# Placing the bias loads later in SyncE's order of loads, dilated stage of a four-block network, one core

## What is computed

```python
proj = (h @ w_in).reshape(B, S, N_DIL_GROUPS, 3, DIL_HEADS, DIL_HEAD_DIM)   # 3 groups, q/k/v, 16 heads, 64
for gi, (window, dilation) in enumerate(((128, 1), (512, 4), (2048, 16))):
    q = rms_norm(proj[:, :, gi, 0], g_q[gi]); k = rms_norm(proj[:, :, gi, 1], g_k[gi]); v = proj[:, :, gi, 2]
    # inside dilated_group: scores plus a bias gathered from a table by distance, softmax over the window
    s = einsum(q, k) * DIL_HEAD_DIM ** -0.5 + bias
    lse = logsumexp(s); p = exp(s - lse); o = einsum(p, v)
o = sum over the groups of softmax(lse over the groups) * o
y = o.reshape(B, S, 1024) @ w_o
```

## Time and profile before

| | us |
|---|---|
| median of 3 runs | 3462.44 |
| lowest and highest | 3458.5, 3465.23 |
| the profiled execution | 3470.18 |
| its span on the core | 3468.1 |
| PE busy in the span | 3271.7 (94%) |
| dilated stage, 826 to 1431 us of the span: PE busy | 574.05 of 605.00 |

### The profile page before, as it was taken

The page is one execution under the profiler, slowest core; times in us unless marked ns, Lnnn a source line. Parts: engine busy times, 40 slices in busy tenths (PEclk is TensorE's granted clock), DMA queues, the critical chain, the costliest instruction groups (busy, mean ns, idle before and its releaser), DMA issues.

```text
span 3468.1 us, 60606 instructions
## 1 busy us (share of the span) xinstructions
PE 3271.7 (94%) x24316; PEld 2519.5 (73%) x24316; DVE 1967.9 (57%) x2468; ACT 1259.1 (36%) x2175; POOL 1276.5 (37%) x729
## 2 busy tenths in 40 slices
PE   6899999999999989999999998888899999999998
PEld 4455678887766767778888887666578787578877
DVE  8457566555464555655554675555466455854444
ACT  3345331224554555531223434333322224242222
POOL 0134434444655544334443322000245443034443
PEclk9999999999999999999999999888999999999999
DMA  6424145443434333244443221000155343023332
GB/s 239 123 89 128 49 135 192 155 168 111 124 110 118 110 88 98 73 152 169 157 169 91 67 62 48 10 13 19 32 188 193 128 157 111 13 81 96 96 91 84
DMA packets 281139, 376.33 MB, mean 109 GB/s; under 512 B 59830, under 2 KB 208987, under 8 KB 269659
## 3 DMA queue, kind: packets, MB, share of 16 engines
q1 hardware_dynamic: 276568, 359.31, 32.8%
q10 hardware_dynamic: 4354, 13.98, 1.0%
HBM read 357.49 MB, written 15.73 MB: 108 GB/s over the span
## 4 chain that ended last, share of the span: by engine, by line
PE 73%; issue 8%; DVE 7%; POOL 3%; DVEq 2%; ACT 2%; DMA 1%; SPq 0%; ACTq 0%; POOLq 0%
PE ps L522 12%; PE ps L523 12%; PE ps L526 12%; POOL w_lo L510 3%; PE ps L1887 2%; PE ps L1889 2%; PE ps L1888 2%; PE ps L1178 1%; PE ps L2872 1%; PE ps L2873 1%; PE ps L2874 1%; PE ps L1094 1%; PE ps L1917 1%; PE ps L1918 1%; PE ps L1919 1%
## 5 line engine op out<-in xcount | busy, mean ns | idle before, releaser
L510 POOL TENSOR_TENSOR w_lo<-w_raw,w_hi 128x1024 fp32r<-128x1024 f32 x288 | 711.4, 2471 | 1036.2 <-ACT w_hi L501 1036.2
L522 PE MATMUL ps<-h_hi,w_hi 128*128 128x512 f32 x2304 | 905.0, 393 | 37.5 <-ACT h_hi L710 13.1
L523 PE MATMUL ps<-h_hi,w_lo 128*128 128x512 f32 x2304 | 902.4, 392 | 0.0
L526 PE MATMUL ps<-h_lo,w_hi 128*128 128x512 f32 x2304 | 823.8, 391 | 0.0
L501 ACT ACTIVATE w_hi<-w_raw 128x1024 fp32r<-128x1024 f32 x288 | 306.0, 1063 | 1092.4 <-PE ps L526 1056.4
L522 PEld LDWEIGHTS ps<-h_hi,w_hi 128*128 128x128 f32 x2304 | 436.1, 189 | 137.8 <-issue 26.4
L523 PEld LDWEIGHTS ps<-h_hi,w_lo 128*128 128x128 f32 x2304 | 436.2, 189 | 90.4
L526 PEld LDWEIGHTS ps<-h_lo,w_hi 128*128 128x128 f32 x2304 | 435.0, 189 | 90.9
L1814 POOL TENSOR_TENSOR w_lo<-w_raw,w_hi 128x512 fp32r<-128x512 f32 x208 | 271.3, 1318 | 329.6 <-ACT w_hi L2080 327.3
L864 DVE TENSOR_TENSOR h_lo<-big,h_hi 128x512 fp32r<-128x512 f32 x100 | 243.2, 2432 | 229.5 <-ACT h_hi L501 229.4
L663 DVE SCALAR_TENSOR_TENSOR big<-yT,cond,big 128x2048 f32<-128x2048 f32 x63 | 176.5, 2801 | 88.1 <-DMA yT<-in_ada_w 87.7
(11 more groups left out here) (518 smaller groups left out, 5474.9 us busy)
## 6 DMA issues: line engine op xcount, KB each, us to landing
w_raw<-in_mlp_w SPq DMA_DIRECT2D x128, 512.0 KB, 3.6
yT<-in_ada_w SPq DMA_DIRECT2D x56, 1024.0 KB, 5.8
w_raw<-in_dil_w_in SPq DMA_DIRECT2D x192, 256.0 KB, 3.1
w_raw<-in_ffn_w_up SPq DMA_DIRECT2D x176, 256.0 KB, 3.0
h_free<-in_ada_w SPq DMA_DIRECT2D x24, 1024.0 KB, 5.0
w_raw<-in_ffn_w_down SPq DMA_DIRECT2D x44, 512.0 KB, 3.6
w_raw<-in_ab_w_in SPq DMA_DIRECT2D x70, 256.0 KB, 2.9
yT<-in_ada_w SPq DMA_DIRECT2D x32, 512.0 KB, 6.2
```

What stands on the lines that cost most here:

```text
L510: self.nc.gpsimd.tensor_tensor(self.w_lo[:, s, :], self.w_raw[:, s, :], self.w_hi[:, s, :].bitcast(F32), ALU.subtract).then_inc(sg["w_spli ...
L522: self.nc.tensor.matmul(out, w_hi, h_hi, start=start, stop=False)
L523: self.nc.tensor.matmul(out, w_lo, h_hi, start=False, stop=False)
L526: return self.nc.tensor.matmul(out, self.w_hi[:, s, lo:lo + P], self.h_lo[:, h, :], start=False, stop=stop)
```

## The change

The SP loop of `dilated` is written anew; no other engine's instructions change. In group 0 the first two weight loads and the first bias stay, but all weight loads of the iteration except the last two go ahead of the second bias. In groups 1 and 2 four weight loads, not two, go ahead of the iteration's bias. The number of DMAs, their sizes and their waits are as they were.

```diff
--- before.py
+++ after.py
@@ -1767,16 +1767,18 @@
             for p in range(24):
                 g, j = divmod(p, 8)
                 until = min(first_unit[p + 1] + 6, len(units))
-                for n in range(done, min(done + 2, until)):
+                ahead = min(done + (2 if SU[g] == 2 else 4), until)
+                for n in range(done, ahead):
                     load(n)
                 if su(g, j, 0) + 2 < 32:
                     load_bias(su(g, j, 0) + 2)
                 if SU[g] == 2:
-                    for n in range(done + 2, min(done + 4, until)):
+                    last = max(min(ahead + 2, until), until - 2)
+                    for n in range(ahead, last):
                         load(n)
                     load_bias(su(g, j, 1) + 2)
-                    done = min(done + 2, until)
-                for n in range(min(done + 2, until), until):
+                    ahead = last
+                for n in range(ahead, until):
                     load(n)
                 done = until
             for n in range(done, len(units)):
```

## The result

| | before | changed |
|---|---|---|
| median of 22 runs each, us | 3463.60 | 3453.76 |
| lowest and highest, us | 3455.92, 3482.53 | 3445.61, 3466.77 |
| profiled execution, us | 3470.18 | 3453.09 |

The ratio changed to before is 0.9971, with a 95% interval from 0.9961 to 0.9981: 6.6 to 13.5 us less of 3463.6. Forecast was 3453.2 us, in a range from 3450 to 3460. One execution of either kernel scatters by some 5 us about its median, as much as half of the effect, so the traces are compared stretch by stretch and not by their totals.

What follows compares the result with a forecast made beforehand. PE, busy 94% of the span, was taken to bound the kernel. Two stalls, 4.76 + 4.49 = 9.25 us, with moved biases costing zero, came off the 3462.44 us median as 9.2 us: 3453.2 us, range 3450 to 3460.

Steps and rivals of the forecast that it cites:

- The bound: Dilated stage: PE, busy 94%, bounds; its 6.1 us of waits for `w_lo` are nearly all there is to win.
- The two stalls: PE's stretches at units 72 to 75 and 84 to 87 lose their waits, giving back 4.76 and 4.49 us.
- The next constraint named: Group 0, iteration 6: unit 75 is late next; POOL has it by 1062.5, PE wants it at 1065, costing nothing.
- The moved biases, group 0: Iteration 6: POOL waits at most 3 us for slot 15's bias, covered by unit 80's 4.9 us; iteration 7 costs nothing.
- Groups 1 and 2: Load 98 before `exps` comes 0.4 to 1.2 us late, hidden by ACT's 2.37 us of idle time; cost taken as zero.
- The cause: Loads 74 and 86 stood behind second biases that waited for their buffer, with issues of 2.17 and 5.34 us.
- the rule of the Trainium skill: By it slot 17's eight issues would hardly hold load 86, leaving no stall there and a gain of 4.8 us.
- the sum: Gains at units 72 to 75 and 84 to 87, 4.76 + 4.49 = 9.25 us, with nothing deducted for moved biases.
- the rival of the missing clock part: At both stalls only idle time is sure: gain 5.6 us, 3456.8 us; chance 0.32, shared with a 3458.2 us case.

Runs made afterwards that it cites:

- the version with group 0 alone: The changed kernel with groups 1 and 2 put back to the old load order: ratio 0.9983, 3459.28 us against 3466.18 us for the kernel before.

## Why the prediction was right

**The bound.** That the 6.1 us of PE's waits for `w_lo` are what can be won, not ACT's 40.8 us, held: ACT still waits 26.9 us for DMAs, and 21.8 us in the version with group 0 alone, and both take 170.9 us from unit 72 to unit 128.

**The two stalls.** 4.76 and 4.49 us were forecast for this execution; 4.78 and 4.51 went. The next constraint named, unit 75 behind PE's unit 71, came as described: ACT took it 0.1 us after PE was done, and PE used it 2.3 us after POOL's split ended, without a wait.

**The moved biases, group 0.** Slot 15's bias was issued from 1067.60 to 1069.77, behind load 79 as worked out, and POOL's mask waited for it once, 0.27 us, where up to 3 us were allowed for. This is POOL in the changed kernel:

```profile
1075.30 1.29 POOL L1811 TENSOR_TENSOR big<-big 128x512 f32<-128x512 f32 x1
1076.86 1.29 POOL L1811 TENSOR_TENSOR big<-big 128x512 f32<-128x512 f32 x1 [0.27 <-DMA big<-bias]
```

**Groups 1 and 2.** ACT waited 0.63 us for unit 98 where 0.4 to 1.2 were forecast, 0.52 and 0.62 for units 114 and 122, not at all for 106, and idled 2.37 us before `exps` as before. The price was zero, as taken.

**The cause.** The prediction named both the wait for the buffer and the issues. With the wait kept and the bias DMAs moved the stalls were gone as well, so the wait alone was not enough. The prediction gave the issues too much weight: by the estimate above the slower landing makes all of the first stall and most of the second. This bears on the rule of the Trainium skill that it cites from "DMA: Bandwidth & Descriptors", that initiating a DMA takes little beside the DMA itself. The rows do not refute it for one DMA: one issue of slot 17's bias took 0.67 us on average (5.34 us for eight), and the quickest value load of the stage before landed 2.6 us after its issue. What the sum rightly did not take from it is that eight issues in a row cost nothing.

**The clock, mis-sized.** The sum counted two stretches at half clock, 3.6 us, as if every execution had them. They stood behind 5 of 8 such waits. By the eight stretches seen (8.47, 10.49, 10.55 and 9.79 us; 10.22, 8.65, 8.65 and 10.13) less 5.71, the means are 4.1 and 3.7 us, 7.8 us together. Six versions with both stalls gone measured ratios of 0.9971, 0.9983, 0.9982, 0.9980, 0.9977 and 0.9968, on average 0.9977, or 8.0 us. So the typical gain is some 8 us rather than 9.2, and the rival of the missing clock part was true in part. The 9.8 us between the medians lie on the high side of that, and their interval, 6.6 to 13.5 us, holds 8 us. That the forecast fell within 1 us of the median is partly luck.

## What to carry to other kernels

A transfer that waits for its own buffer can delay what is queued behind it in three ways: by the wait, by its issues, and by the slower landing of the next load. Here the wait alone used the slack but for 0.3 to 0.5 us, and the other two made the idle time; so look at the length of the issue rows and at the time from issue to landing of the load behind them, not only at the waits. To size such a change, compare the whole stretch with an undisturbed one of the same work, split the difference into idle time and half clock, and count only the idle time as sure; here the half clock stood behind five of eight such waits. When total times scatter by as much as the gain, compare stretches of the traces, and take a time found in one trace only as one draw.

## What the runs showed of the hardware that was not expected

- Two executions with the same idle times of PE, 2.5 to 3.1 us, differ in what follows: a stretch of 3.41 us at 1.2 GHz in five cases, 2.4 GHz throughout in three.
- A DVE copy of 64 x 1536 within SBUF took 0.95 us when it began just ahead of a POOL subtraction and 1.99 us when it began just behind; POOL's subtraction took 2.07 us instead of 1.27 in the first case. "SBUF — State Buffer" of the Trainium skill, section "Who interferes with whom", says that DVE and GpSimd share one pair of ports, that a DVE copy can run in a mode that takes this pair, and that whoever issues first then holds it for the whole instruction while the other waits. The trace agrees: 0.14 us in the start of POOL's instruction moved PE by 1.0 us.
- The same bias bytes (slot 18) in 16 issues instead of 8 took 8.8 us of SP's time instead of 5.0, 0.55 us for an issue on average instead of 0.62, and the weight load behind them landed 2.9 us after its own issue instead of 4.8 (for the next three slots 3.3 to 3.6 instead of 4.8 to 5.2).
- Bias DMAs ahead of a weight load on the same queue slowed its landing as well as its issue, and four in group 0 slowed it more than eight in group 1: behind four issues of 128 KB, 2.17 us long, the load landed 7.97 us after its own issue, behind eight of 64 KB, 5.34 us long, 4.54 us, and behind none 2.7 and 2.6 us. Over the 13 traces it was 7.0 to 8.1 us behind the four and 4.4 to 5.6 us behind the eight.
